# Attention outputs of a streaming encoder step: who adds the two halves

## The reference

```python
s = jnp.einsum('bqhd,bkhd->bhqk', qi, k, preferred_element_type=jnp.float32) * sc
s = s + (Fi[:, :, :, None] - Ft[:, :, None, :])
s = jnp.where(kpos[None, :] <= qpos[:, None], s, -jnp.inf)
pr = jax.nn.softmax(s, axis=-1)
out = jnp.einsum('bhqk,bkhd->bqhd', pr.astype(v.dtype), v)
z = jnp.concatenate([attn * jax.nn.silu(ag), pool * jax.nn.silu(pg)], axis=-1)
```

## Time and profile before

| | us |
|---|---|
| median of three executions | 1428.19 |
| profiled execution, its own time | 1433.23 |
| its span | 1431.5 |
| TensorE busy | 1298.6 (91%) |
| VectorE busy | 716.8 (50%) |
| ScalarE busy | 569.9 (40%) |
| GpSimd busy | 179.6 (13%) |

### The profile page before, as it was taken

How to read it: one execution, slowest core, us unless ns; L and a number is a source line. 1 busy time by engine, 2 the same in 40 slices (tenths; PEclk the granted TensorE clock), 3 DMA queues, 4 the chain that set the end, 5 groups by cost and what they waited for, 6 DMA issues and landing times. The chain is left out here.

```text
span 1431.5 us, 19348 instructions
## 1 busy us (share of the span) xinstructions
PE 1298.6 (91%) x7007; PEld 1049.6 (73%) x7007; DVE 716.8 (50%) x1973; ACT 569.9 (40%) x1158; POOL 179.6 (13%) x196
## 2 busy tenths in 40 slices
PE   7899999999999999995699989999999991599996
PEld 1779988888888888885576676767767671488884
DVE  1646433244461111000588877888788881334434
ACT  3546411212112121111477676776777670211111
POOL 1213301101001010100000230131032023000000
PEclk9899999999999999998599999999999995799998
DMA  9636344112213434223913655739456413756662
GB/s 365 232 118 195 141 140 127 60 46 76 87 46 126 155 123 142 88 68 97 199 21 57 105 96 122 136 70 173 82 100 105 94 31 104 251 162 192 206 191 88
DMA packets 159644, 179.51 MB, mean 125 GB/s; under 512 B 34073, under 2 KB 123533, under 8 KB 154878
## 3 DMA queue, kind: packets, MB, share of 16 engines
q1 hardware_dynamic: 153294, 155.21, 42.0%
q10 hardware_dynamic: 5824, 21.50, 4.5%
q0 software_dynamic: 432, 1.57, 0.3%
HBM read 111.55 MB, written 66.69 MB: 125 GB/s over the span
## 5 line engine op out<-in xcount | busy, mean ns | idle before, releaser
L597 PE MATMUL prj_acc<-prj_hhi,til_whi 128*128 128x512 f32 (+1 forms) x800 | 286.5, 358 | 0.0
L599 PE MATMUL prj_acc<-prj_hlo,til_whi 128*128 128x512 f32 (+1 forms) x800 | 284.1, 355 | 0.0
L598 PE MATMUL prj_acc<-prj_hhi,til_wlo 128*128 128x512 f32 (+1 forms) x800 | 284.1, 355 | 0.0
L1386 ACT ACTIVATE att_whi<-att_tps 128x512 fp32r<-128x512 f32 x336 | 169.2, 516 | 118.8 <-PE att_tps L1352 116.0
L1416 DVE TENSOR_TENSOR att_wlo<-att_tps,att_whi 128x512 fp32r<-128x512 f32 x336 | 189.9, 584 | 32.1 <-ACT att_whi L1386 31.8
L1406 DVE TENSOR_SCALAR_CACHE_REDUCE att_wx<-att_sps 128x512 f32<-128x512 f32 x192 | 113.4, 619 | 131.0 <-PE att_sps L1337 127.0
L1336 PE MATMUL att_sps<-att_ka,att_qa 128*128 128x512 f32 (+4 forms) x328 | 153.3, 467 | 25.6 <-DMA att_kb<-scratch_fkd 23.7
L599 PEld LDWEIGHTS prj_acc<-prj_hlo,til_whi 128*128 128x128 f32 x800 | 150.8, 189 | 21.4
L597 PEld LDWEIGHTS prj_acc<-prj_hhi,til_whi 128*128 128x128 f32 x800 | 150.8, 189 | 20.9
L598 PEld LDWEIGHTS prj_acc<-prj_hhi,til_wlo 128*128 128x128 f32 x800 | 150.9, 189 | 20.7
L1524 PE MATMUL fin_acc<-fin_whi,fin_zh 128*128 128x512 f32 (+1 forms) x272 | 106.8, 393 | 45.1 <-DMA fin_zl<-scratch_z 45.1
(11 more groups left out here) (182 smaller groups left out, 1915.5 us busy)
## 6 DMA issues: line engine op xcount, KB each, us to landing
til_wraw<-in_w_in SPq DMA_DIRECT2D x20, 512.0 KB, 4.2
att_ka<-scratch_k SPq DMA_DIRECT2D x16, 560.0 KB
scratch_v<-val_vs SPq DMA_DIRECT2D x17, 512.0 KB, 4.4
att_qa<-scratch_q SPq DMA_DIRECT2D x16, 528.0 KB
val_xt<-in_x_prompt ACTq DMA_DIRECT2D x16, 512.0 KB, 4.4
ini_al<-in_w_ada SPq DMA_DIRECT2D x8, 1024.0 KB, 15.7
fin_zh<-scratch_z SPq DMA_DIRECT2D x16, 512.0 KB, 4.4
fin_zl<-scratch_z SPq DMA_DIRECT2D x16, 512.0 KB, 5.8
```

The source lines that it names most:

```text
L597: pe.matmul(out, w[0][:, k, :], hhi[:, k, cs], start=(k == 0), stop=False)
L598: pe.matmul(out, w[1][:, k, :], hhi[:, k, cs], start=False, stop=False)
L599: mm = pe.matmul(out, w[0][:, k, :], hlo[:, k, cs], start=False, stop=(k == KT - 1))
L1386: act.activation(whi[x.i % W_RING][0:x.keys, x.skip:x.width], tps[x.i % T_RING][0:x.keys, x.skip:x.width], ACT.Copy).then_inc(hi_ok, 1)
```

## The change

ScalarE copies all 128 partitions of the bank to tmp, then waits for its own copy and, from pair 1 on, for the gate product that last read these columns of att; then it issues a transfer of 64 partitions from the low half of tmp to the main half of att. GpSimd takes every output: it waits for the transfer, adds tmp's main half to att in place, and only then goes on with the gate at odd heads. TensorE's bank is free when the copy is done. VectorE has no event for an output.

```diff
--- before.py
+++ after.py
@@ -1216,10 +1216,11 @@
         ops = [s.ps(f"ops{n}", [P, 512]) for n in range(O_RING)]
         qk_in = [s.sem(f"qk_in{e}") for e in range(2)]
         v_in = [s.sem(f"v_in{e}") for e in range(2)]
-        names = ("s_full", "s_free", "row_ok", "exp_ok", "t_full", "hi_ok", "lo_ok", "val_ok", "low_out", "out_ok",
+        names = ("s_full", "s_free", "row_ok", "exp_ok", "t_full", "hi_ok", "lo_ok", "val_ok", "copied", "out_ok",
                  "den_sum", "rec_ok", "ag_in", "g_mul", "g_hi", "g_z", "g_lo")
-        (s_full, s_free, row_ok, exp_ok, t_full, hi_ok, lo_ok, val_ok, low_out, out_ok,
+        (s_full, s_free, row_ok, exp_ok, t_full, hi_ok, lo_ok, val_ok, copied, out_ok,
          den_sum, rec_ok, ag_in, g_mul, g_hi, g_z, g_lo) = (s.sem(n) for n in names)
+        low_in = [s.sem(f"low_in{n}") for n in range(O_RING)]
         rd_out, rb_in, z_out = ([s.sem(f"{n}{e}") for e in range(2)] for n in ("rd_out", "rb_in", "z_out"))
         QK, V = 16 * 10, 16 * 3
         NS = len(ORDER) + 1
@@ -1356,7 +1357,7 @@
                     if x is STEPS[4 * h].units[0]:
                         pe.wait_ge(v_in[e], V * (h // 2 + 1))
                     if x.first and x.out.i >= O_RING:
-                        pe.wait_ge(out_ok, x.out.i - O_RING + 1)
+                        pe.wait_ge(copied, x.out.i - O_RING + 1)
                     pe.wait_ge(lo_ok, x.i + 1)
                     bank = ops[x.out.i % O_RING]
                     b = x.i % W_RING
@@ -1391,7 +1392,11 @@
                     act.wait_ge(val_ok, st.units[-1].i + 1 if x is st.outs[-1] else st.units[-3].i + 1)
                     if x.i >= O_RING:
                         act.wait_ge(out_ok, x.i - O_RING + 1)
-                    act.activation(tmp[main, b, 0:x.width], ops[b][low, 0:x.width], ACT.Copy).then_inc(low_out, 1)
+                    act.activation(tmp[:, b, 0:x.width], ops[b][:, 0:x.width], ACT.Copy).then_inc(copied, 1)
+                    if st.pair >= 1:
+                        act.wait_ge(g_lo, gates(x) - NS + 1)
+                    act.wait_ge(copied, x.i + 1)
+                    act.dma_start(att[main, x.cols], tmp[low, b, 0:x.width]).then_inc(low_in[b], 16)
 
         @block.vector
         def _(dve):
@@ -1415,14 +1420,6 @@
                     dve.wait_ge(hi_ok, x.i + 1)
                     dve.tensor_tensor(wlo[b][0:x.keys, x.skip:x.width], tps[x.i % T_RING][0:x.keys, x.skip:x.width],
                                       raw(whi[b][0:x.keys, x.skip:x.width]), ALU.subtract).then_inc(lo_ok, 1)
-                elif kind == "out":
-                    b = x.i % O_RING
-                    main, _ = halves(e)
-                    dve.wait_ge(low_out, x.i + 1)
-                    if st.pair >= 1:
-                        dve.wait_ge(g_lo, gates(x) - NS + 1)
-                    dve.tensor_tensor(att[main, x.cols], ops[b][main, 0:x.width], tmp[main, b, 0:x.width],
-                                      ALU.add).then_inc(out_ok, 1)
                 elif kind == "den":
                     r = slice(4 * x.c, 4 * x.c + 4)
                     dve.wait_ge(exp_ok, x.pieces[-1].i + 1)
@@ -1438,6 +1435,13 @@
         @block.gpsimd
         def _(pool):
             for out in OUTS:
+                b, (main, _) = out.i % O_RING, halves(out.step.e)
+                done = NS * out.step.pair + (gates(out) % NS if out.step.e else 0)
+                if done:
+                    pool.wait_ge(g_lo, done)
+                pool.wait_ge(low_in[b], 16 * (out.i // O_RING + 1))
+                pool.tensor_tensor(att[main, out.cols], att[main, out.cols], tmp[main, b, 0:out.width], ALU.add).then_inc(out_ok, 1)
+                pool.wait_ge(out_ok, out.i + 1)
                 if out.step.e == 0:
                     continue
                 pair, cols = out.step.pair, out.cols
@@ -1446,7 +1450,6 @@
                 pool.wait_ge(ag_in, 16 * (pair + 1))
                 pool.wait_ge(rb_in[n % 2], 32 * (n // 2 + 1))
                 pool.tensor_tensor(ag[:, cols], ag[:, cols], rb[:, cols], ALU.mult).then_inc(g_mul, 1)
-                pool.wait_ge(out_ok, out.i + 1)
                 pool.wait_ge(g_mul, n + 1)
                 if n >= 2:
                     pool.wait_ge(z_out[n % 2], 32 * (n // 2))
```

## The result

The changed kernel takes 1438.56 us (median of 14 runs, 1434.81 to 1444.88), the kernel before 1429.02 (14 runs on the same chip, 1426.02 to 1434.45): a ratio of 1.0064, 95% interval 1.0049 to 1.0079, 9 us slower. The forecast was 1436.3. The profiled execution took 1441.04 us with a span of 1439.2, 7.7 more than the span before.

A forecast was written before the change was run, and what follows sets the result against it. TensorE was taken to bound attention, then a chain of queues the seam to the last stage. Terms -2.3 + 6.2 + 3.7 + 0.5 = +8.1 us gave 1436.3 us against the median 1428.2; range 1427 to 1448.

The forecast's parts named there:

- VectorE's adds, -2.3: Attention, first output of each head: without the add, low halves come 0.3 us earlier, 8 heads, -2.3 us; bounds 0 to -5.5.
- ScalarE's copy, 0: ScalarE's output copies: 128 partitions instead of 64 take the same time, since time goes by columns; 0 us.
- ScalarE's wait and issue, +6.2: ScalarE's queue in attention: 0.45 us more per output delays exps behind second and third outputs, +6.2 us; bounds 0 and 12.5.
- The 3.1 at second outputs: Second output of 7 heads: ScalarE has no gap before the exp TensorE waits for, 0.45 us each, 3.1 us.
- The 3.1 at third outputs: Third output of 7 heads: eight exps follow the copy and TensorE waits for the last, 0.45 us each, 3.1 us.
- The transfer, 1.8: 128 KB from tmp to att: lands in 1.8 us like a store from SBUF, 3.7 kept for the range.
- GpSimd's add first, +3.7: Last pair: multiplication stands behind the add, so z stores and last reciprocals leave 3.7 us later; bounds 0 and 5.6.
- The last add, +0.46: Sample's output, 64 columns, between the last two gate products on GpSimd: 0.32 and a wait of 0.14, +0.46 us.
- A: Rival: ScalarE's gaps absorb its extra 0.45, or reciprocals return as early as today; about 1432 us; chance 0.27.
- B: Rival: TensorE's clock stays up behind third outputs, 7 heads give back 24 us, 1412 us; chance 0.11.
- C: Rival: a second fall of TensorE's clock behind the second output, 27 us more, 1463 us; chance 0.08.
- D: Rival: ScalarE's issue stands behind SyncE's v loads in heads 1 to 6, 32 us more, 1468 us; chance 0.04.

The follow-up runs named there:

- relief: Kernel before without VectorE's 40 adds; ScalarE copies the main half straight to att, low half of outputs left out; 3.5 us faster by the median (0.24%).
- after_mult: Changed kernel with GpSimd's multiplication of the gate put ahead of its add; ratio 1.0083 to the kernel before.
- the early order: SyncE stores the last head's reciprocals as soon as VectorE has them: changed kernel 1.0025; changed kernel with two copies, no transfer, 0.9973; kernel before 0.9973.
- the broadcasts ahead: Early order with the third step's broadcasts ahead of the last reciprocals' store, in three kernels; misses in time, no ratios given in the text.
- issue: Kernel before, where ScalarE also waits for its own copy and sends it to a tile nobody reads; 0.32% slower.
- two_copies: Changed kernel without the transfer: ScalarE copies both halves into the same partitions, GpSimd adds them; ratio 0.9995 to the kernel before.
- after_rec: Changed kernel; SyncE stores the last step's reciprocals before the second output's z instead of behind it; ratio 1.0068 to the kernel before.
- after_order: Changed kernel, early stores, third step's broadcasts ahead of the last store, SyncE awaiting a transfer's landing before each of the last two stores; no ratio given.

## Why the prediction was right and where it was not

The time was right, 1436.3 against 1438.56, by luck: two sums that were each 8 us off cancelled. Step by step:

- *VectorE's adds, -2.3.* Too small, and the bound of -5.5 too. The relief alone makes the first stretch of odd heads 0.93 and the second 0.61 shorter (even heads 0.8 and 0.34), about -10 together, and none of it at third outputs of odd heads. The step that failed is "At the other outputs no low half right behind the add ends a wait that I can count on": at the second outputs the 0.24 stall for exps was the trace of a chain that began with the add. The list of waits shows only the last link.
- *ScalarE's copy, 0.* Right: 0.59 as before.
- *ScalarE's wait and issue, +6.2.* The 3.1 at second outputs were 0.0 to 0.1 a head. The 3.1 at third outputs were right in place and a little small, 7 x 0.58 = 4.1, because the wait and the issue (0.47, not 0.33) cost 0.58 and not 0.45. Both terms together made attention 4 us longer; it was 4.5 shorter.
- *The transfer, 1.8.* Wrong: 8.2 us where it mattered. I took the landing from stores of the projection stage, and didn't ask what SyncE has in flight at that moment, though the earlier trace rows hold the reciprocals' stores whose landing GpSimd waits 11.45 us for.
- *GpSimd's add first, +3.7.* The mechanism was right to the link, z stores behind the add, reciprocals behind the z stores; the size was not. Of what was missing, 6.4 us are the transfer's 8.2 in place of 1.8. The reciprocals leave 10.5 us later against the end of attention (9.7 from the copy to the z stores, some 1 from the third output that now comes sooner after the second), and their landing takes 1.1 longer.
- *The last add, +0.46.* As far as the rows tell: add at 1214.53, multiplication at 1214.92, 0.39; of it 0.1 is left at PE's start (29.9 against 29.8).
- *Sum.* -2.3 + 6.2 in attention was -4.5; +3.7 + 0.5 in the tail was +12.0. The errors, 8.4 and 7.8 us, cancelled.

The rivals: A (half absorbed) held for the second outputs. B and C did not come: the dips of the clock stand as before (0.75 and 0.59 in the stretches above, 0.72 and 0.60 before). D fell: ScalarE's issue at 791.64 took 0.47 us in the midst of SyncE's v load, which took its queue from 782.62 to 797.59. The rule of exclusive use (the Trainium skill, Perfetto Trace Analysis, section "DMA Instruction — HWDGE (DVE, Sync)") isn't borne out for ScalarE by this 0.47; what the load delays is the landing.

## What to carry to other kernels

Price a transfer by what the other queues have in flight when it is issued, above all stores of single elements, and not by its size: here the same 128 KB took 2.3 or 8.2 us. Measure an engine's relief in stretches between two fixed events of the loop, since the list of waits shows only the last link of a chain. And where the end hangs on one queue, write down its order with the landing of each entry: making attention's stretches some 10 us shorter gained 3.5; the tail's chain of stores and landings kept its own pace, and waits for key loads may have taken more.

## What the runs showed of the hardware

- A landing is held by another queue's store of 4-byte elements: 2.3 us free of it, 8.2 with one store in flight, 13.3 between two. In after_mult it is the completion alone that waits (rows moved within 2 us, add after 7.9).
- Within SyncE's v load ScalarE's issue takes 0.47 us, but the transfer issued at 791.64 can be added only at 801.22, 9.6 us later, 3.6 after that load's issue ended. Here the data wait too: its rows move at 798.5 to 799.8.
- From the store of the third step's reciprocals until SyncE, which waits for its landing, goes on: 11.0 to 11.5 us in the six profiles where z stores follow it at once or 3 us later (those of the early order and of the broadcasts ahead), 8.7 to 10.8 in the eight others, where they precede it.
- One stall is open. At 838 to 844 us ScalarE and VectorE stand for 2.5 to 6 us; PE waits 2.06 us in the changed kernel, 5.25 in relief, 3.59 in issue, 4.11 in two_copies, 4.36 in after_rec and 3.12 in after_order. The other eight profiles, with and without the change, have none there. It wasn't tried further.

```profile
838.48 0.60 ACT L1387 ACTIVATE att_whi<-att_tps 128x512 fp32r<-128x512 f32 x1 [3.40 <-remote]
839.97 0.74 PE L1353 MATMUL att_tps<-keep_ident,att_wx 128*128 128x128 f32 x4 [2.06 <-DVE att_wlo L1421]
```
